# Split weights moved by a few words each, and sixteen strips that run through their tokens backwards

## The reference

```python
def hybrid_layer(x, ...):                        # first layer
    h = rms_norm(x, norm1_w)
    (rq, rk, rv, rg, dq, dk, dv, cb, cc, cx, gates) = [h @ w_in[:, s:e] for s, e in column_bounds()]
    ret = head_layer_norm(retention(rq, rk, rv)) * silu(rg)
    diff = diff_attention(dq, dk, dv, ...)
    conv = cb * short_conv(cc * cx, conv_w)
    g = sigmoid(gates)
    x = x + (g[0] * (ret @ w_branch[0]) + g[1] * (diff @ w_branch[1]) + g[2] * (conv @ w_branch[2])) @ w_out
    return x + square(relu(rms_norm(x, norm2_w) @ w_up)) @ w_down

# second layer: the same frame with other parts
    proj = rmsnorm(h) @ w_in
    mix = (gate_sb * (stick_breaking(...) @ w_sb_out) + gate_gla * (gla(...) @ w_gla_out)) @ w_o
    h = h + rmsnorm(mix)
    act = gelu(causal_dwconv(rmsnorm(h) @ w_ffn_up))
    h = h + rmsnorm((act * (rmsnorm(h) @ w_ffn_gate)) @ w_ffn_down)
```

## Time and profile before

| | |
|---|---|
| median of 3 runs | 2102.3 us |
| the profiled execution | 2102.32 us, span 2100.5 us |
| TensorE matmuls busy | 2087.2 us, 13662 of them |
| VectorE busy | 1244.4 us |
| ScalarE busy | 831.4 us |
| GpSimd busy | 164.4 us |
| DMA | 203.36 MB, mean 97 GB/s |

### The profile page before, as it was taken

How to read it: one execution, slowest core, us unless ns; L and a number is a source line. 1 busy time by engine, 2 the same in 40 slices (tenths; PEclk the granted TensorE clock), 3 DMA queues, 4 the chain that set the end, 5 groups by cost and what they waited for, 6 DMA issues and landing times.

```text
span 2100.5 us, 33898 instructions
## 1 busy us (share of the span) xinstructions
PE 2087.2 (99%) x13662; PEld 1850.4 (88%) x13662; DVE 1244.4 (59%) x1847; ACT 831.4 (40%) x1305; POOL 164.4 (8%) x146
## 2 busy tenths in 40 slices
PE   9999999999999999999999999999999999999998
PEld 8998988898888788899898888999999998889897
DVE  6775444565555555777665666367855567546364
ACT  4333222433444443434434566343424344222233
POOL 0012000030000000232120000022300000000000
PEclk9999999999999999999999999999999999999999
DMA  4343221522222233332323221231133222322322
GB/s 151 111 167 114 86 76 61 199 82 83 73 68 71 96 106 99 109 111 81 110 91 100 81 92 60 82 122 59 54 140 105 91 80 91 97 94 90 100 91 100
DMA packets 53563, 203.36 MB, mean 97 GB/s; under 512 B 6960, under 2 KB 7344, under 8 KB 52288
## 3 DMA queue, kind: packets, MB, share of 16 engines
q1 hardware_dynamic: 49248, 177.56, 26.3%
q10 hardware_dynamic: 3232, 20.80, 2.5%
q0 software_dynamic: 960, 3.24, 0.5%
HBM read 190.96 MB, written 10.62 MB: 96 GB/s over the span
## 4 chain that ended last, share of the span: by engine, by line
PE 93%; DVE 4%; ACT 2%; issue 0%; DMA 0%; SPq 0%; DVEq 0%; ACTq 0%
PE ps L2174 69%; PE ps L2297 7%; PE ps L2773 5%; PE ps L2639 1%; PE ps L2421 1%; PE ps L2446 1%; PE ps L2374 1%; PE ps L2705 1%; PE ps L2545 1%; DVE kk_r L1827 1%; PE ps L2460 1%; ACT kk L966 1%; ACT kk L967 1%; PE ps L2683 0%; PE ps L2526 0%; PE ps L2353 0%
## 5 line engine op out<-in xcount | busy, mean ns | idle before, releaser
L556 ACT ACTIVATE wh<-wraw 128x1024 fp32r<-128x1024 f32 x284 | 300.3, 1057 | 730.7 <-PE ps L2174 612.5
L1234 DVE TENSOR_TENSOR wl<-wraw,wh 128x1024 fp32r<-128x1024 f32 x298 | 365.6, 1228 | 132.6 <-ACT wh L556 129.0
L2174 PE MATMUL ps<-xh,wh 128*128 128x264 f32 (+1 forms) x1800 | 325.3, 325 | 0.6 <-DVE tmp L1267 0.5
L2174 PE MATMUL ps<-xl,wh 128*128 128x264 f32 (+1 forms) x1800 | 317.2, 321 | 0.0
L2174 PE MATMUL ps<-xh,wl 128*128 128x264 f32 (+1 forms) x1800 | 316.8, 320 | 0.0
L2174 PEld LDWEIGHTS ps<-xh,wh 128*128 128x128 f32 x1800 | 264.4, 188 | 30.1 <-issue 2.4
L2174 PEld LDWEIGHTS ps<-xl,wh 128*128 128x128 f32 x1800 | 265.2, 188 | 25.7
L2174 PEld LDWEIGHTS ps<-xh,wl 128*128 128x128 f32 x1800 | 265.2, 188 | 25.3
L2174 PE MATMUL ps<-bh,wh 128*128 128x264 f32 (+1 forms) x1296 | 231.7, 322 | 0.3 <-ACT wh L556 0.2
L2174 PE MATMUL ps<-bl,wh 128*128 128x264 f32 (+1 forms) x1296 | 227.9, 319 | 0.0
L2174 PE MATMUL ps<-bh,wl 128*128 128x264 f32 (+1 forms) x1296 | 227.8, 319 | 0.0
(11 more groups left out here) (532 smaller groups left out, 2776.8 us busy)
## 6 DMA issues: line engine op xcount, KB each, us to landing
wraw<-weights_dram SPq DMA_DIRECT2D x299, 512.0 KB, 3.6
qq<-weights_dram SPq DMA_DIRECT2D x12, 512.0 KB, 4.5
kk<-weights_dram SPq DMA_DIRECT2D x12, 512.0 KB, 4.4
hf<-tables_dram POOLq DMA_DIRECT2D x12, 264.0 KB, 3.0
res<-x_t_dram SPq DMA_DIRECT2D x4, 528.0 KB, 7.2
res<-x_t_dram ACTq DMA_DIRECT2D x1, 2112.0 KB, 9.2
res_dram<-res ACTq DMA_DIRECT2D x1, 2112.0 KB, 6.4
mrg_dram<-mrg ACTq DMA_DIRECT2D x1, 2112.0 KB, 8.7
```

The source lines that it names most:

```text
L556: nc.scalar.activation(wh[:, slot], wraw[:, slot], ACT.Copy).then_inc(hi_done, 1)
L1234: nc.vector.tensor_tensor(wl[:, slot], wraw[:, slot], wh[:, slot].bitcast(F32), ALU.subtract)\
L2174: last = nc.tensor.matmul(o, w[:, slot, c, :], a[:, c, tok], start=(k == 0), stop=(k == len(steps) - 1))
```

## The change

A table `PLACE` gives each strip a place in words of 4 bytes, by which its eight chunks are moved within the slot, in both `wh` and `wl`. The slots grow by 64 words. `split_hi`, `split_lo` and all matmuls of strips take the operand through `strip_at`. Where the number of a strip is a loop's expression, the place is that of the loop's first turn, which `Slot` carries along. A place of 62 words is 248 bytes, 8 less than 256, and so on: apart from conv_in and gla_gates the moves are 4 to 80 bytes up or down, counted modulo 256. In `strip`, sixteen strips (gla_gates and ffn3up) read the moving operand and write PSUM with a negative step. The last two turns of two loops over splits stand outside their loops.

```diff
+PLACE, REVERSED = [0] * NSTRIP, [False] * NSTRIP
+for _name in ("ret_qkv", "diff_qkv", "sb_main", "sb_proj", "gla_lr", "gla_main", "gla_gates"):
+    for _n in range(dict(PHASES)[_name]):
+        PLACE[START[_name] + _n] = (0, 2, 62, 4, 60, 6, 12, 20, 44, 58, 50, 10, 1, 63)[_n % 14]
+for _n in range(8):
+    REVERSED[START["gla_gates"] + _n] = REVERSED[START["ffn3up"] + _n] = True
+    PLACE[START["gla_gates"] + _n] = 8 * _n
+for _k in range(24):
+    PLACE[START["conv_in"] + _k] = (3, 14, 2, 28, 36, 62)[_k % 6]
+for _k in range(8):
+    PLACE[START["gla_proj"] + _k] = PLACE[START["w_o"] + _k] = (0, 52)[_k % 2]
+for _g in range(4):
+    for _k in range(16):
+        PLACE[START[f"ffn{_g}up"] + _k] = ((2, 62), (4, 60), (1, 63), (0, 16))[_g][_k % 2]
...
-    return base + k + step * i, (base + k) // 2 + (step // 2) * i, (base + k) % 2
+    return base + k + step * i, (base + k) // 2 + (step // 2) * i, Slot(base + k)
...
+class Slot(int):
+    def __new__(cls, first):
+        slot = int.__new__(cls, first % 2)
+        slot.first = first
+        return slot
...
+def strip_at(w, n, slot):
+    o = PLACE[n if isinstance(n, int) else slot.first]
+    return w[:, int(slot), o:o + KC * P].rearrange("p (k n) -> p k n", k=KC)
...
-        wh, wl = sb("wh", [P, 2, KC, P], F32R), sb("wl", [P, 2, KC, P], F32R)
+        wh, wl = (sb(n, [P, 2, KC * P + 64], F32R) for n in ("wh", "wl"))
...
-        st_w = ([wh[:, k].rearrange("p k n -> p (k n)") for k in range(2)] + [flat(vtr)[:, 4 * D:5 * D]],
-                [wl[:, k].rearrange("p k n -> p (k n)") for k in range(2)] + [flat(xrowsr)[:, 0:D]])
+        st_w = ([wh[:, k, 0:KC * P] for k in range(2)] + [flat(vtr)[:, 4 * D:5 * D]],
+                [wl[:, k, 0:KC * P] for k in range(2)] + [flat(xrowsr)[:, 0:D]])
...
-                nc.scalar.activation(wh[:, slot], wraw[:, slot], ACT.Copy).then_inc(hi_done, 1)
+                nc.scalar.activation(strip_at(wh, n, slot), wraw[:, slot], ACT.Copy).then_inc(hi_done, 1)
...
-                with act.Fori(0, count // 2) as i:
+                with act.Fori(0, count // 2 - 1) as i:
                     for j in range(2):
                         split_hi(*pos(B, j + 1, i))
+                for k in (count - 1, count):
+                    split_hi(*pos(B, k))
...
-                nc.vector.tensor_tensor(wl[:, slot], wraw[:, slot], wh[:, slot].bitcast(F32), ALU.subtract)\
+                nc.vector.tensor_tensor(strip_at(wl, n, slot), wraw[:, slot], strip_at(wh, n, slot).bitcast(F32), ALU.subtract)\
...
-                        last = nc.tensor.matmul(o, w[:, slot, c, :], a[:, c, tok], start=(k == 0),
+                        back = REVERSED[number if isinstance(number, int) else slot.first]
+                        x = a[:, c, tok]
+                        last = nc.tensor.matmul(o[:, ::-1] if back else o, strip_at(w, number, slot)[:, c, :],
+                                                x[:, ::-1] if back else x, start=(k == 0),
                                                 stop=(k == len(steps) - 1))
```

More of the change, by code:

```diff
@@ L585, in _ @@
                     act.wait_ge(w_loaded[0], 16)
-                    nc.scalar.activation(wh[:, 0, 0:2], wraw[:, 0, 0:2], ACT.Copy).then_inc(first_hi, 1)
+                    nc.scalar.activation(strip_at(wh, 0, 0)[:, 0:2], wraw[:, 0, 0:2], ACT.Copy).then_inc(first_hi, 1)
                 if c == 1:
-                    nc.scalar.activation(wh[:, 0, 2:KC], wraw[:, 0, 2:KC], ACT.Copy).then_inc(hi_done, 1)
+                    nc.scalar.activation(strip_at(wh, 0, 0)[:, 2:KC], wraw[:, 0, 2:KC], ACT.Copy).then_inc(hi_done, 1)
             n_hi += KC
@@ L1278, in _ @@
                     dve.wait_ge(first_hi, 1)
-                    nc.vector.tensor_tensor(wl[:, 0, 0:2], wraw[:, 0, 0:2], wh[:, 0, 0:2].bitcast(F32), ALU.subtract)\
+                    nc.vector.tensor_tensor(strip_at(wl, 0, 0)[:, 0:2], wraw[:, 0, 0:2],
+                                            strip_at(wh, 0, 0)[:, 0:2].bitcast(F32), ALU.subtract)\
                         .then_inc(first_lo, 1)
@@ L1282, in _ @@
                     dve.wait_ge(hi_done, 1)
-                    nc.vector.tensor_tensor(wl[:, 0, 2:KC], wraw[:, 0, 2:KC], wh[:, 0, 2:KC].bitcast(F32), ALU.subtract)\
+                    nc.vector.tensor_tensor(strip_at(wl, 0, 0)[:, 2:KC], wraw[:, 0, 2:KC],
+                                            strip_at(wh, 0, 0)[:, 2:KC].bitcast(F32), ALU.subtract)\
                         .then_inc(lo_done, 1)
@@ L2096, in _ @@
                 B = START[f"glu{g}down"]
-                with dve.Fori(0, n_g // 2) as i:
+                with dve.Fori(0, n_g // 2 - 1) as i:
                     for j in range(2):
                         split_lo(*pos(B, j + 1, i))
+                for k in (n_g - 1, n_g):
+                    split_lo(*pos(B, k))
                 for t in range(4):
@@ L2196, in product @@
                             (ps[:, 2 * p[2], :], slice(NM, T))
-                        ins = nc.tensor.matmul(o, w[:, p[2], c, :], a[:, c, tok], start=(c == 0 and w is wh and a is xh),
+                        ins = nc.tensor.matmul(o, strip_at(w, p[0], p[2])[:, c, :], a[:, c, tok], start=(c == 0 and w is wh and a is xh),
                                                stop=(c == KC - 1 and a is xl))
@@ L2249, in first_strip @@
                         for k in range(2):
-                            last = nc.tensor.matmul(ps[:, k, 0:HALF], w[:, 0, c, :], a[:, c, HALF * k:HALF * k + HALF],
+                            last = nc.tensor.matmul(ps[:, k, 0:HALF], strip_at(w, 0, 0)[:, c, :], a[:, c, HALF * k:HALF * k + HALF],
                                                     start=(c == 0 and w is wh and a is xh),
@@ L2587, in strip_by_halves @@
                         for c in range(KC):
-                            last = nc.tensor.matmul(ps[:, k, 0:HALF], w[:, slot, c, :],
+                            last = nc.tensor.matmul(ps[:, k, 0:HALF], strip_at(w, n, slot)[:, c, :],
                                                     a[:, c, HALF * k:HALF * k + HALF], start=(w is wh and a is bh and c == 0),
@@ L2638, in _ @@
                             for k in range(2):
-                                last = nc.tensor.matmul(ps[:, z + k, 0:HALF], w[:, slot, 4 * o + c, :],
+                                last = nc.tensor.matmul(ps[:, z + k, 0:HALF], strip_at(w, n, slot)[:, 4 * o + c, :],
                                                         a[:, c, HALF * k:HALF * k + HALF],
@@ L2767, in chunk_products @@
             def chunk_products(g, c, n_g, tiles, w, a, halves_of=(0, 1)):
-                slot = (START[f"glu{g}down"] + c) % 2
+                n = START[f"glu{g}down"] + c
+                slot = n % 2
                 for t in tiles:
@@ L2773, in chunk_products @@
                         last = nc.tensor.matmul(ps[:, 2 * t + h, :], a[:, c, NM + P * t:NM + P * t + P],
-                                                w[:, slot, 4 * h:4 * h + 4, :].rearrange("p k n -> p (k n)"),
+                                                strip_at(w, n, slot)[:, 4 * h:4 * h + 4, :].rearrange("p k n -> p (k n)"),
                                                 start=first, stop=(c == n_g - 1 and w is wl), skip_group_check=True)
```

## The result

| | before | after |
|---|---|---|
| median | 2102.3 us | 2115.85 us (3 runs, 2115.75 to 2115.85) |
| ratio | | 1.0064, 95% interval 1.005 to 1.0078 |
| span of the profiled execution | 2100.5 us | 2114.0 us |

The change costs 13.55 us. The forecast was slower, 2110 us, within 2082 to 2160. The direction and the range held; the working did not hold in all its terms, as the experiments show, and two of its errors covered each other.

What follows compares the result with a forecast made beforehand. The prediction took the start-to-start distance of TensorE's matmuls to bound the kernel. It added +2.8 us for places and +5.0 for finely shifted starts, +7.8 on 2102.3, giving 2110 us, range 2082 to 2160.

Steps and rivals of the forecast that it cites:

- What bounds the kernel: Whole kernel: TensorE, busy 2087.2 of 2100.5 us; the start-to-start distance of successive matmuls sets the end, not waits.
- Nothing: Rival for all moved strips: places cancel or read ports are independent, within 4 us of 2102; chance 0.14.
- Part 1, S strips: New weight places in 56 strips of 512 tokens: -2.2 ns on each of 1344 matmuls, -3.0 us.
- the 16 ns of the earlier trace: Time beyond the columns' own per matmul in L2558, taken as upper bound for moved strips.
- middle of rows: For all moved strips: 11.2 ns beyond the columns' time per matmul, between bounds of 6.4 and 16 ns.
- Part 1, T strips: New weight places in 100 strips of 528 tokens: +1.2 ns on each of 4800 matmuls, +5.8 us.
- Part 2, finely shifted starts: Strips at places not divisible by four words: 1.3 ns x 2400 + 2.5 ns x 768 matmuls, +5.0 us.
- Part 3, backwards: Sixteen strips in gla_gates and ffn3up read and write backwards: taken as 0.
- Half rate: Rival in gla_gates and ffn3up: backward strips run at half rate, +90 us, 2200 us; chance 0.10.
- Parts 4 and 5: Splits writing wh and wl off their place: cost 0, at worst a few us; peeling two loops' last splits: nothing.
- the readers fall out of step: Rival in moved strips: places that differ lower the time per matmul, 2076 to 2098 us; chance 0.28.

Runs made afterwards that it cites:

- e7: Kernel before with the weights of all strips but the second layer's down strips 64 bytes on, tokens unmoved, forwards: 2135.77 us (+33.5).
- e8: Kernel before with tokens and weights both 64 bytes on, the second layer's down-strip weights unmoved, forwards: 2106.13 us (+3.8).
- e5: Kernel before with the weights of all strips but the second layer's down strips one word (4 bytes) on, tokens unmoved: 2126.87 us (+24.6).
- e1: Changed kernel with only the strips of 512 columns moved (56 strips, 1344 matmuls), none backwards: 2108.67 us, +6.5 over the kernel before.
- e2: Changed kernel with only the strips of 264 columns moved (100 strips, 4800 matmuls), none backwards: 2108.58 us, +6.4 over the kernel before.
- e10: Kernel before, but the second half of each 264-column pair reads from the 256th token instead of the 264th: 2117.16 us (+14.9).
- e9: Changed kernel with the same phases moved only by multiples of 4 words, forwards: 2114.86 us, +12.6 over the kernel before.
- e4: Kernel before with tokens and weights both one word (4 bytes) on, the second layer's down-strip weights unmoved, forwards: 2165.6 us (+63.5).
- e6: Kernel before with the tokens one word (4 bytes) on, all weights unmoved, forwards: 2165.9 us (+63.6).

## Why the forecast was right and where it was not

**What bounds the kernel**: right. TensorE's starts are the span, and a nanosecond on each is in it at once. The waits stayed where they were, and pieces with place 0 did not move by 0.01 us. That the distance between the readers matters was right too (e7 against e8). The rule that the forecast takes from the Trainium skill, "TensorE: Matmul & The Clock Gate", step by step, is that loading the next weights takes nothing from the running matmul. By it moving the weights alone would cost nothing; the runs have 24.6 us for it in e5 and 33.5 in e7, and the forecast's "Nothing" rival falls with them. Through what the two reads meet is not shown.

**Part 1, S strips: wrong in sign.** -3.0 us was forecast, +6.5 measured (e1), at 233 ns on most places. The step that failed is the reading of agreement as the bad case, since L2297 runs at 120.0 ns with it and 113.1 without; for 512 columns it is the best case, 227.4 ns against 231 to 234 at most places. The rows were thin as well: over all of L2297 the two relations are 3 ns apart and not 7. I also took the 16 ns of the earlier trace rows for an upper bound; the surplus goes to 233.4 - 213.3 = 20 ns, and to 236.7 - 213.3 = 23 with shifted tokens. The middle of rows that come from other lines and widths was no estimate for this one.

**Part 1, T strips: right in sign and size, with luck.** +5.8 us forecast, +6.4 measured (e2), 1.3 ns on each of 4800 matmuls against 1.2. The figure is the same middle of rows that fails for the S strips, and e10 shows that the distance it rests on does not set a T matmul's price alone.

**Part 2, finely shifted starts: no such term for the weights.** +5.0 us was charged to places off four words. e9 has none of them and costs 12.6 us, and in the table the fine places (232.4, 230.8, 233.4 and 233.5 ns for S strips) cost no more than the coarse ones. For tokens a fine start does cost, some 10 ns on an S matmul whatever the weights do (e4, e6), more than the 8 ns that I took for the upper end; the change does not move tokens.

**Part 3, backwards: taken as 0, is not.** 6.5 ns on an S matmul, 25.1 us over all strips. In the change it adds little, 0.6 to 0.85 us beyond e1 and e2, since most of the sixteen strips are off place 0 anyway and the two costs are alternatives: backwards at place 16 takes 233.3 ns, at place 0 233.4. Half rate is out.

**Parts 4 and 5: right at 0.** Splits of 1057 and 1225 ns, waits of 0.5 us, unchanged pieces.

So the sum of 7.8 us was 5.8 too low. Of its three terms one was right, one had the wrong sign (9.5 us off), and one, +5.0 us for fine starts, measured nothing and by luck made up for half of that error. Without it the same working would have said 2105 us. The rival "the readers fall out of step", with 2076 to 2098 us, had the mechanism backwards for S strips: leaving the common start costs.

**Left open**: which part of the memory or of TensorE's read sets these numbers; why 16 bytes down costs 1 to 2 ns and 16 up 6; why agreement is best at 512 columns and not at 256 or 264. A row of 512 columns is 2048 bytes, a multiple of 256, so its start and its end agree with the weights together, and no run tells which of the two counts. For narrower rows, where the row before ended may count too; e10 hints at it, and no run tests it.

## What to carry to other kernels

Where TensorE is busy throughout and, as here, loads float32r weights for each matmul of 512 columns, give weights and moving rows starts that agree modulo 256 bytes. If they have to move by 64 bytes, move both; do not let a moving row begin a word off, which moving the weights along did not mend. For 256 and 264 columns agreement was not the best, and no place tried beat the one they had by more than 0.3 ns for both halves together. A few nanoseconds on 6144 matmuls were 13 us here. Read a matmul's price from start to start at the very width and places in question, and over more than one short stretch: a better figure from another width pointed the wrong way twice (part 1 and e10). For the strips here a negative step was free on the write to PSUM and cost as much as a bad place on the read.

## What the hardware showed that I had not expected

A moving row of 512 columns that begins 4 bytes off takes 236.7 ns from start to start in place of 226.7, and shifting the weights along does not help (237.8), while at 64 bytes shifting them along restores 54.62 us for 240 matmuls. Reading backwards at full clock takes 233.4 ns, writing backwards no more than forwards. Two halves of 264 columns that begin at the same byte modulo 256 take 120.1 and 125.0 ns in e10. The surplus of an S matmul is not a smooth function of the place: 227.5 to 228.7 ns at 60, 229.1 at 48, 230.8 at 2, 231.1 at 58 and 230.0 at 44 (22 matmuls each), and 232 to 234 at all others measured.
